# Padding TensorE's instruction stream ahead of the two loops of an expert layer: no-ops in place of a branch, and one more alignment

## The reference, cut to what matters

```python
n = rmsnorm(x) ; P = n @ W_in
h = x + W_out [ rwkv7(P_r) || mamba2(P_m) ]
h = h + peer_ffn(rmsnorm(h))        # the part around the change
y = rmsnorm_final(h)

# peer_ffn: 8 heads pick 16 of 16384 experts for each token
hid = einsum('td,ted->te', x, u_tab[eid])
out = einsum('te,ted->td', gelu(hid) * gate, v_tab[eid])
```

## Time and profile before

| | us |
|---|---|
| median of three executions | 2712.46 |
| lowest, highest | 2710.13, 2712.49 |
| the profiled execution's own time | 2710.13 |
| its span, from the first to the last instruction | 2708.1 |
| TensorE matmuls busy (share of the span) | 2508.3 (93%) |
| TensorE weight loads busy | 2445.5 (90%) |
| VectorE, ScalarE, GpSimd busy | 1549.5, 968.0, 651.9 |
| mean granted TensorE clock, as a share of full speed | 0.953 |

### The profile page before, as it was taken

One profiled execution on the slowest core, in us unless ns is written; L12 is line 12 of the kernel. 1 busy time (PEld: TensorE's weight loads), 2 busy tenths in 40 slices (PEclk: granted clock), 3 DMA queues, 4 the chain that ended last, 5 costly groups with the idle time before them and its releaser, 6 DMA issues. The chain is left out here.

```text
span 2708.1 us, 48006 instructions
## 1 busy us (share of the span) xinstructions
PE 2508.3 (93%) x18910; PEld 2445.5 (90%) x18910; DVE 1549.5 (57%) x2800; ACT 968.0 (36%) x1818; POOL 651.9 (24%) x313
## 2 busy tenths in 40 slices
PE   7977888897899899899979999999999999999997
PEld 6975778787799899888879999999999999999997
DVE  4334554633678777588745454454454454777775
ACT  3334344422333232688853222222222222222222
POOL 2433343423154545111112221221221220000000
PEclk9997899868999999999989999999999999999999
DMA  5331000003133233365674332332332332544551
GB/s 183 110 104 47 24 24 1 13 1 129 58 106 97 89 97 106 115 178 173 192 232 138 113 109 95 111 111 95 109 113 96 106 113 77 171 171 165 186 176 40
DMA packets 162451, 296.11 MB, mean 109 GB/s; under 512 B 11872, under 2 KB 99232, under 8 KB 158120
## 3 DMA queue, kind: packets, MB, share of 16 engines
q1 hardware_dynamic: 162344, 294.61, 33.1%
HBM read 230.26 MB, written 64.31 MB: 109 GB/s over the span
## 5 line engine op out<-in xcount | busy, mean ns | idle before, releaser
L117 PE MATMUL banks<-w_high,v_low 128*128 128x288 f32 x2048 | 604.5, 295 | 0.0
L115 PE MATMUL banks<-w_high,v_high 128*128 128x288 f32 x2048 | 603.6, 295 | 0.4
L116 PE MATMUL banks<-w_low,v_high 128*128 128x288 f32 x2048 | 603.0, 294 | 0.0
L115 PE MATMUL banks<-res_hi,u_high 128*128 128x288 f32 x1440 | 428.2, 297 | 10.9 <-ACTq L2002 10.9
L117 PE MATMUL banks<-res_hi,u_low 128*128 128x288 f32 x1440 | 425.5, 296 | 0.0
L116 PE MATMUL banks<-res_lo,u_high 128*128 128x288 f32 x1440 | 425.2, 295 | 0.0
L115 PEld LDWEIGHTS banks<-w_high,v_high 128*128 128x128 f32 x2048 | 384.2, 188 | 3.7 <-DVE w_low L1972 3.7
L116 PEld LDWEIGHTS banks<-w_low,v_high 128*128 128x128 f32 x2048 | 384.2, 188 | 0.0
L117 PEld LDWEIGHTS banks<-w_high,v_low 128*128 128x128 f32 x2048 | 384.1, 188 | 0.0
L1996 DVE TENSOR_TENSOR res_x<-banks,res_x 128x288 f32<-128x288 f32 x512 | 225.0, 454 | 267.2 <-PE banks L117 267.2
L1618 POOL TENSOR_TENSOR u_low<-u_raw,u_high 128x1024 fp32r<-128x1024 f32 x72 | 183.7, 2552 | 706.2 <-ACT u_high L1614 706.2
(11 more groups left out here) (327 smaller groups left out, 4471.5 us busy)
## 6 DMA issues: line engine op xcount, KB each, us to landing
v_raw<-arg_v SPq DMA_DIRECT2D x128, 512.0 KB, 3.8
scratch_gates<-gate_stage SPq DMA_DIRECT2D x18, 2048.0 KB, 9.3
u_raw<-arg_u SPq DMA_DIRECT2D x36, 1024.0 KB, 6.2
gates_in<-scratch_gates SPq DMA_DIRECT2D x32, 1152.0 KB, 7.1
q_raw<-arg_u SPq DMA_DIRECT2D x38, 512.0 KB, 3.6
scratch_hidden<-gelu_ahead SPq DMA_DIRECT2D x56, 288.0 KB, 2.5
gelu_out<-scratch_hidden SPq DMA_DIRECT2D x56, 288.0 KB, 2.8
in_raw<-arg_w_in SPq DMA_DIRECT2D x25, 512.0 KB, 3.9
```

Source lines behind the costliest of these rows:

```text
L115: pe.matmul(out, ah, bh, start=first, stop=False)
L116: pe.matmul(out, ah, bl, start=False, stop=False)
L117: return pe.matmul(out, al, bh, start=False, stop=last)
```

## The change

The directive ahead of the first loop loses its `max_nops=0`, so that its pad slots are executed as no-ops and not branched over. A second directive of the same kind is put between group 17 and the second loop, where there was none. Both are emitted for TensorE alone. Nothing is computed in another way.

```diff
                 whole(eng, 0, 0, first=True, last=False)
                 if align:
-                    eng.addr_align(align, max_nops=0)
+                    eng.addr_align(align)
                 with eng.Fori(0, NH // 2 - 1) as it:
                     whole(eng, it * 2 + 1, 1, first=False, last=False)
                     whole(eng, it * 2 + 2, 0, first=False, last=False)
                 whole(eng, NH - 1, 1, first=False, last=True)
+                if align:
+                    eng.addr_align(align)
                 with eng.Fori(0, (NG - NH) // 2) as it:
                     loaded(eng, it * 2 + NH, 0)
                     loaded(eng, it * 2 + (NH + 1), 1)
```

## The result

The changed kernel takes 2727.28 us (median), the kernel before 2712.47. The ratio is 1.0057, with a 95% interval of 1.004 to 1.0075, so it is slower, by 10.8 to 20.3 us at the interval's ends. The profiled executions have spans of 2722.8 and 2708.1 us, 14.7 us apart.

A forecast was written before the change was run, and what follows sets the result against it. TensorE, its weight loads busy nearly throughout, was taken to set the time around both directives. Second-directive stall 12.8, slow clock 2.9 and first-directive stall 1.3 summed to 17.0 us, added to 2712.46 for 2729.5 us; range 2718 to 2739.

The forecast's parts named there:

- The count of pads: On TensorE's sequencer: about 41 pads at the first directive (span 25 to 41) and 188 at the second.
- the sum: Whole kernel: 12.8 + 2.9 + 1.3 = 17.0 us slower, 2729.5 us; pads alone at the second directive 14.7 us.
- The price of a pad: On TensorE's sequencer: a NOP takes 0.078 us, 0.07 around it plus 0.008 of work; bounds 0.008 and 0.12.
- The rival of cheap pads: No-ops dropped at queueing rate, up to 0.03 us a pad, so time stays within 0.2%; chance 0.11.
- The lead: Ahead of the second loop the sequencer is 1.84 us ahead of TensorE's array; that much of the pads costs nothing.
- The stall: At the second loop's entry the array stands still 12.8 us: 188 pads' 14.7 us less the 1.84 us lead.
- The clock: Behind the second directive's stall the granted clock stays at 0.50 for some 6 us, costing 2.9 us more.
- The first directive: Ahead of the first loop: 41 pads, 3.2 us, less 1.55 lead and 0.37 branch, stall 1.3 us, clock stays.
- saves nothing: Second loop's alignment: fetching is not repeated, and its body touches 4 blocks from slot 69 or slot 1.
- alignment pays: Second loop waits for instructions now; aligning wins several us, or 1.6 us if only branches count (2710.9); chance 0.02.

The follow-up runs named there:

- after: The changed kernel: first directive without max_nops=0 and a second directive ahead of the second loop, against the kernel before; 2727.28 us against 2712.47, ratio 1.0057.
- a2_second_only: Kernel before plus only the second directive, its 188 pads executed; the first directive keeps its branch; 2728.09 us, ratio 1.0052.
- a4_no_directive: Kernel before with its directive removed, so neither loop is aligned; 2735.14 us against 2712.54, ratio 1.0069.
- a3_both_branched: Kernel before plus the second directive with max_nops=0, so its 188 pads are branched over; 2714.63 us against 2712.54, ratio 1.0001.
- c4_second_loop_five_blocks: Kernel before plus a branched second directive of offset 220, so the second loop's body touches 5 blocks; 2713.21 us against 2711.04, ratio 0.9998.
- b1_pads24: Kernel before plus a second directive whose offset leaves 24 executed pads ahead of the second loop; 2710.77 us, ratio 1.0005.
- b2_pads48: Kernel before plus a second directive whose offset leaves 48 executed pads ahead of the second loop; 2712.75 us, ratio 1.0004.
- before: The kernel without the change: first directive with max_nops=0, its pads branched over, and no second directive; median 2712.47 us.
- c2_head_190: Kernel before with the first directive at offset 190, branch kept, so the first loop's body touches 7 blocks; ratio 1.0001.
- b4_late_head: Kernel before with the first directive at offset 222, branch kept, so the first loop's body touches 8 blocks; ratio 1.0085.
- c3_head_204: Kernel before with the first directive at offset 204, branch kept, so the first loop's body touches 8 blocks; ratio 1.0079.
- b3_pads100: Kernel before plus a second directive whose offset leaves 100 executed pads ahead of the second loop; 2718.36 us, ratio 1.0026.

## Why the prediction was right

**The count of pads** was right, 41 and 188. The 188 came from the slots between two MOVEs (256 - 68), and the 41 from the distance between a fetch packet and the branch. The 41 was in part luck: 14.1 / 0.065 is 217 slots and not 215, which leaves 39 pads, and 41 is the top of the span of 25 to 41 that the prediction gave. No row of before shows that a directive without `max_nops` executes as many as 188 pads, on which the 14.7 us of the sum rest; the runs show 188 NOPs for it (`after`, `a2_second_only`), and no run has a larger count.

**The price of a pad** was 0.078 us in the prediction and is 0.073. The step from the sequencer's other instructions to the NOP held: the record shows work (13 ns, forecast 8), and 0.06 us lie around it (forecast 0.07), two errors that partly cancel. The rival of cheap pads needed 0.03 us a pad or less, by which `a2_second_only` would have lost at most 5.4 us, and it lost 14.

**The lead** was put at 1.84 us ahead of the second loop. By the pads that stay free, 26, it is 1.9, and by the changed kernel's own entry 188 x 0.073 - 11.85 = 1.9. The stall was 12.8 us in the sum and is 11.85, by the price of a pad alone.

**The clock** was put at 2.9 us and cost 2.0. The term was taken from the gap at 1395 us, after which the clock was at half for 6 us more; after the gap at 2300 it was so for 4.3 us. This was the weakest term, as neither the fall nor the return of the clock is set by the gap's length alone (the 2.7 us in `a4_no_directive` without a fall): 5.4 us of idle loads cost 2.3 us and 11.8 us cost 2.0.

**The first directive** was put at 1.3 us and cost 1.1. Its clock stayed, as forecast.

The sum was 17.0 us; the medians lie 14.8 us apart and the spans 14.7. All three terms were somewhat too large, and none had the wrong sign or was missing.

**Where the reasoning was too short.** The prediction said of alignment that fetching is not repeated, and went from there to "saves nothing". For the second loop this is shown (`a3_both_branched`, `c4_second_loop_five_blocks`). For the first loop the rows of before could not show it, as they were taken with the alignment in place: with it no packet lies inside the loop and without it 63 do (`a4_no_directive`), and it is worth some 20 us. The forecast did not suffer, since both kernels align the first loop. The rival "alignment pays" was priced as if only crossings or a branch of 0.2 us could cost; what the runs show is a branch back of 4 us (3966 to 4026 ns) where the body touches 8 blocks, and 814 slots touch 5 at most.

## What to carry to other kernels

Count how long no-ops keep the sequencer busy and how far it is ahead: here they took 0.073 us each against a lead of some 2 us, and behind stalls of 5.4 and 11.8 us the slow clock cost 2.3 and 2.0 us as well. Pads ahead of a busy loop should be branched over (`max_nops=0`; here 188 of them then cost nothing, to 0.1 us) or put where the engine waits anyway (127 cost nothing there). Before a loop is aligned, count the blocks that its body touches with and without it: here 7 or 4 or 5 made no difference, and 8 cost some 20 us, so of the two loops only the first has a use for a directive.

## What the runs showed of the hardware

A NOP on TensorE's sequencer has a record of 13 ns and takes 73 ns from start to start (`after`, `a2_second_only`). TensorE's sequencer was some 1.9 us ahead of its array in a dense stream of matmuls: 24 pads made no gap (`b1_pads24`), 48 one of 1.6 us (`b2_pads48`), and the line through the longer gaps reaches zero at 26. The loop of 1595 slots was fetched once when its body touched 7 blocks of 256 slots (`before`, `c2_head_190`), and again at each of its 7 branches back when it touched 8, 9 packets of 16 KB a branch, with 4.0 us in the branch in place of 0.2 (`a4_no_directive`, `b4_late_head`, `c3_head_204`). The granted clock stayed at full speed behind idle gaps of the weight loads of 1.0 us (`after`) and 1.6 us (`b2_pads48`), and fell to 0.50 behind those of 5.4 us (`b3_pads100`) and 11.8 us (`after`). In between the length did not decide: of seven gaps of 1.6 to 2.7 us in `a4_no_directive` it fell behind those of 2.2 and 2.1 us and stayed behind the longest.
